# Where a wide expert unit's first two weight pieces land, and when they are transferred

## The reference

```python
def _swiglu(x, w_gate, w_up, w_down):
    return (jax.nn.silu(x @ w_gate) * (x @ w_up)) @ w_down

def _moe(h, w_router, w_gate, w_up, w_down):
    logits = (x @ w_router).astype(jnp.float32)
    top_v, top_i = lax.top_k(logits, TOP_K)          # TOP_K = 2 of 8 experts
    gates = jax.nn.softmax(top_v, axis=-1)
    combine = ...                                     # gate of each token and expert
    for e in range(N_EXPERTS):
        out = out + combine[:, e:e + 1] * _swiglu(x, w_gate[e], w_up[e], w_down[e])
```

## Time and profile before

| | us |
|---|---|
| median of three runs | 1407.58 (1405.72 to 1408.84) |
| the profiled execution's own time | 1405.3 |
| its span | 1403.5 |
| TensorE busy | 1325.2 (94%) |
| VectorE busy | 875.6 (62%) |
| ScalarE busy | 724.1 (52%) |
| mean transfer rate over the span | 314 GB/s, 440.55 MB |

### The profile page before, as it was taken

One profiled execution on the slowest core, in us unless ns is written; L12 is line 12 of the kernel. 1 busy time (PEld: TensorE's weight loads), 2 busy tenths in 40 slices (PEclk: granted clock), 3 DMA queues, 4 the chain that ended last, 5 costly groups with the idle time before them and its releaser, 6 DMA issues.

```text
span 1403.5 us, 19596 instructions
## 1 busy us (share of the span) xinstructions
PE 1325.2 (94%) x7528; PEld 1031.4 (73%) x7528; DVE 875.6 (62%) x954; ACT 724.1 (52%) x719; POOL 69.6 (5%) x92
## 2 busy tenths in 40 slices
PE   9999999999999999999997889998779998888997
PEld 8999999999999778888852258872238884226786
DVE  6554766544987699988830168860128881017897
ACT  7564544344566777777720057750027771006775
POOL 0100000000000063000000000000000000002000
PEclk9999999999999999999999999999999999999999
DMA  8563553553442799999989999989999999999992
GB/s 315 194 224 120 180 180 121 193 183 108 175 166 69 276 343 380 421 407 406 372 317 421 421 407 421 416 339 387 421 420 407 421 359 356 421 421 420 421 421 105
DMA packets 75877, 440.55 MB, mean 314 GB/s; under 512 B 7296, under 2 KB 9344, under 8 KB 30672
## 3 DMA queue, kind: packets, MB, share of 16 engines
q1 hardware_dynamic: 71680, 422.67, 76.4%
q0 software_dynamic: 3952, 16.49, 3.3%
q10 hardware_dynamic: 144, 0.02, 0.0%
HBM read 433.12 MB, written 11.01 MB: 316 GB/s over the span
## 4 chain that ended last, share of the span: by engine, by line
PE 72%; DMA 13%; DVE 7%; issue 4%; ACT 3%; SPq 0%; DVEq 0%; ACTq 0%
PE ps L2235 9%; PE ps L2236 9%; PE ps L2241 8%; DMA raw<-in_moe_w_gate 8%; PE ps L2360 7%; PE ps L1740 4%; PE ps L2259 4%; PE ps L2267 4%; PE ps L2260 4%; PE ps L1730 4%; PE ps L1731 4%; DMA raw<-in_moe_w_up 3%; PE ps L1778 2%; PE ps L1795 2%; PE ps L1779 2%
## 5 line engine op out<-in xcount | busy, mean ns | idle before, releaser
L1427 DVE TENSOR_TENSOR wl<-raw,wh 128x2048 fp32r<-128x2048 f32 x180 | 410.9, 2290 | 62.5 <-ACT wh L880 61.5
L880 ACT CAST wh<-raw 128x2048 fp32r<-128x2048 f32 x180 | 344.3, 1914 | 144.7 <-PE ps L2236 57.2
L2235 PE MATMUL ps<-wh,gh 128*128 128x512 f32 x560 | 222.0, 396 | 11.5 <-issue 8.4
L2236 PE MATMUL ps<-wh,gl 128*128 128x512 f32 x560 | 220.6, 394 | 0.0
L2360 PE MATMUL ps<-raw,few 128*64 128x512 f32 x288 | 139.3, 633 | 37.1 <-issue 28.7
L2362 PE MATMUL ps<-raw,few 128*64 128x512 f32 x312 | 155.8, 650 | 0.0
L2241 PE MATMUL ps<-wl,gh 128*128 128x512 f32 x560 | 151.3, 392 | 0.2 <-DVE wl L1427 0.2
L944 ACT ACTIVATE sil<-ps 64x512 f32<-64x512 f32 x21 | 12.4, 588 | 261.6 <-PE ps L2362 261.6
L2235 PEld LDWEIGHTS ps<-wh,gh 128*128 128x128 f32 x560 | 106.2, 190 | 37.3 <-issue 13.5
L2360 PEld LDWEIGHTS ps<-raw,few 128*64 128x64 f32 x288 | 39.2, 145 | 120.0 <-issue 120.0
L2236 PEld LDWEIGHTS ps<-wh,gl 128*128 128x128 f32 x560 | 106.2, 190 | 23.0
(11 more groups left out here) (353 smaller groups left out, 2378.2 us busy)
## 6 DMA issues: line engine op xcount, KB each, us to landing
raw<-in_moe_w_gate SPq DMA_DIRECT2D x101, 1024.0 KB, 11.3
raw<-in_moe_w_up SPq DMA_DIRECT2D x99, 1024.0 KB, 10.6
raw<-in_moe_w_down SPq DMA_DIRECT2D x88, 1024.0 KB, 12.1
raw_more<-in_moe_w_down SPq DMA_DIRECT2D x24, 1024.0 KB, 10.7
raw_more<-in_moe_w_up SPq DMA_DIRECT2D x13, 1024.0 KB, 14.1
raw<-in_diff_w_qkv SPq DMA_DIRECT2D x8, 1536.0 KB, 6.1
raw_more<-in_moe_w_gate SPq DMA_DIRECT2D x11, 1024.0 KB, 7.3
raw<-in_sb_w_qkv SPq DMA_DIRECT2D x7, 1536.0 KB, 7.7
```

Source lines behind the costliest of these rows:

```text
L880: act.copy(split_piece(wh, p), raw_piece(p)).then_inc(wh_ready, 1)
L1427: dve.tensor_tensor(split_piece(wl, p), raw_piece(p), raw_f(split_piece(wh, p)), ALU.subtract).then_inc(wl_ready, 1)
L2235: pe.matmul(ps[:, bank, :], gh[:, s], w, start=(k0 + k == 0), stop=False)
L2236: ins = pe.matmul(ps[:, bank, :], gl[:, s], w, start=False, stop=False)
```

## The change

The unused quarters of `wh` and `wl` get a second name, `unsplit`, by which float32 data can be written there. The first two pieces of each wide unit but the very first are transferred into them (`spare(0)` in `wh`, `spare(1)` in `wl`), with semaphores of their own (`spare_landed`). For the wide units behind small ones, the two transfers are issued by `load_few`, right behind its pieces 37 and 39, with no wait; pieces 2 to 41 still go to the raw slots. The counts of landings for each slot are changed to match. For the second wide unit the two are issued once the expert's number is known.

```diff
+        def splits(own):
+            return sb("wh", [P, 2, CHUNK], F32R, where=own), sb("wl", [P, 2, CHUNK], F32R, where=own)
+        wh, wl = phase(splits)
+        unsplit = phase(lambda own: sb("unsplit", [P, 2, 2, CHUNK], where=own))
...
+        def wide_piece(a, p, first=False):
+            if p < EARLY and not first:
+                return spare(p), spare_landed[p]
+            return raw_piece(p), piece_landed[p % RAW_SLOTS]
...
+            def load_early(a, e, p):
+                kind, i = unit_chunks[p // 2]
+                to, landed_ = wide_piece(a, p)
+                source = weights_of[kind][bass.ds(e * (FC * 2 * P) + P * (2 * i + p % 2), P), :]
+                sp.dma_start(to, source).then_inc(landed_, 16)
             def load_wide(a, e, few_before):
-                for p in range(PIECES):
+                for p in range(EARLY, PIECES):
                     kind, i = unit_chunks[p // 2]
                     if few_before is not None and p < RAW_SLOTS:
                         sp.wait_ge(few_used, few_before * PIECES + PIECES + p + 1 - RAW_SLOTS)
-                    else:
+                    elif p < RAW_SLOTS or p >= RAW_SLOTS + EARLY:
                         sp.wait_ge(wl_ready, a * PIECES + C_MOE + p + 1 - RAW_SLOTS)
                     load_piece(e, p, kind, i, p % 2)
-            def load_few(v, e):
+            def load_few(v, e, after):
...
                     load_piece(e, p, kind, i, half)
+                    if p in after:
+                        load_early(v + 1, after[p][0], after[p][1])
+            def early(e):
+                return {PIECES - 5: (e, 0), PIECES - 3: (e, 1)}
...
             with sp.Fori(1, len(SMALL_UNITS) + 1) as v:
-                load_few(v, sp.value_load(bm["unit_i"][0:1, bass.ds(2 * v, 1)], ...))
-                load_wide(v + 1, sp.value_load(bm["unit_i"][0:1, bass.ds(2 * v + 1, 1)], ...), v)
+                few_e = sp.value_load(bm["unit_i"][0:1, bass.ds(2 * v, 1)], ...)
+                next_e = sp.value_load(bm["unit_i"][0:1, bass.ds(2 * v + 1, 1)], ...)
+                load_few(v, few_e, early(next_e))
+                load_wide(v + 1, next_e, v)
...
-            def unit_split(u, a, p, first=False):
-                act.wait_ge(piece_landed[p % RAW_SLOTS], piece_in(u, p))
+            def unit_split(few, a, p, first=False):
+                piece, landed_ = wide_piece(a, p, first)
+                act.wait_ge(landed_, wide_in(a, few, p, first))
...
-                act.copy(split_piece(wh, p), raw_piece(p)).then_inc(wh_ready, 1)
+                act.copy(split_piece(wh, p), piece).then_inc(wh_ready, 1)
```

More of the change, by code:

```diff
@@ L95 @@
 RAW_SLOTS, SPLIT_SLOTS = 7, 3
+EARLY = 2
 MAX_UNITS = E + 4
@@ L293, in build @@
         piece_landed = [sem(f"piece_landed{i}") for i in range(RAW_SLOTS)]
+        spare_landed = [sem(f"spare_landed{i}") for i in range(EARLY)]
         wh_ready, wl_ready = sem("wh_ready"), sem("wl_ready")
@@ L406, in split_piece, with spare, landed_before, wide_in @@
             return w[:, slot // 2, slot % 2 * PIECE:(slot % 2 + 1) * PIECE]
-        def piece_in(u, p):
-            return u * (16 * PIECES // RAW_SLOTS) + 16 * (p // RAW_SLOTS + 1)
+        def spare(n):
+            return unsplit[:, n, SPLIT_SLOTS // 2, SPLIT_SLOTS % 2 * PIECE:(SPLIT_SLOTS % 2 + 1) * PIECE]
+        def wide_piece(a, p, first=False):
+            if p < EARLY and not first:
+                return spare(p), spare_landed[p]
+            return raw_piece(p), piece_landed[p % RAW_SLOTS]
+        def landed_before(slot, a, few):
+            rounds = PIECES // RAW_SLOTS
+            return 16 * rounds + 16 * (rounds - (1 if slot < EARLY else 0)) * (a - 1) + 16 * rounds * few
+        def wide_in(a, few, p, first=False):
+            if first:
+                return 16 * (p // RAW_SLOTS + 1)
+            if p < EARLY:
+                return 16 * a
+            slot = p % RAW_SLOTS
+            return landed_before(slot, a, few) + 16 * (p // RAW_SLOTS + (0 if slot < EARLY else 1))
+        def few_in(a, few, p):
+            return landed_before(p % RAW_SLOTS, a, few) + 16 * (p // RAW_SLOTS + 1)
         def split_free(a, p, first):
@@ L513, in _ @@
                     e = sp.value_load(bm["unit_i"][0:1, bass.ds(a + len(SMALL_UNITS), 1)], min_val=0, max_val=E - 1)
+                    for p in range(EARLY):
+                        load_early(a, e, p)
                     load_wide(a, e, None)
@@ L900, in _ @@
                          ps[:, BACKS[n], :]).then_inc(back_ev, 1)
-            unit_split(0, 0, 1)
+            unit_split(0, 0, 1, first=True)
             def gathered_high(k):
@@ L921, in _ @@
             gathered_high(1)
-            unit_split(0, 0, 2)
+            unit_split(0, 0, 2, first=True)
             def few_gathered(v):
@@ L979, in unit_body @@
                     if 2 * j + 3 < PIECES:
-                        unit_split(u, a, 2 * j + 3)
+                        unit_split(few, a, 2 * j + 3, first)
                     if kind == "d" and i + 1 < FC:
@@ L983, in unit_body @@
                     if 2 * j + 4 < PIECES:
-                        unit_split(u, a, 2 * j + 4)
+                        unit_split(few, a, 2 * j + 4, first)
                     if (kind, i) == ("g", 1):
@@ L1424, in unit_split @@
                 dve.wait_ge(wh_ready, a * PIECES + C_MOE + p + 1)
-                dve.wait_ge(w_used, split_free(a, p, first))
-                dve.tensor_tensor(split_piece(wl, p), raw_piece(p), raw_f(split_piece(wh, p)),
+                dve.wait_ge(w_used, split_free(a, p, first and p == 0))
+                dve.tensor_tensor(split_piece(wl, p), wide_piece(a, p, first)[0], raw_f(split_piece(wh, p)),
                                   ALU.subtract).then_inc(wl_ready, 1)
@@ L1493, in _ @@
             gathered_low(1, (0,))
-            unit_split(0, 1)
+            unit_split(0, 1, first=True)
             gathered_low(1, (1,))
-            unit_split(0, 2)
+            unit_split(0, 2, first=True)
             def sort_experts():
@@ L1635, in unit_body @@
                     if 2 * j + 3 < PIECES:
-                        unit_split(a, 2 * j + 3)
+                        unit_split(a, 2 * j + 3, first)
                     if kind == "u":
@@ L1648, in unit_body @@
                     if 2 * j + 4 < PIECES:
-                        unit_split(a, 2 * j + 4)
+                        unit_split(a, 2 * j + 4, first)
                     if stored and 8 <= j < 16:
```

51 lines of the change are left out of this document (27 added, 24 removed).

## The result

The changed kernel takes 1424.49 us (median of four runs, 1423.43 to 1425.19); the kernel before took 1407.57. The ratio is 1.0121, 95% interval [1.0103, 1.0138]: 16.9 us slower. Forecast were 1420 and a range of 1411 to 1425. The profiled execution took 1423.43 us with a span of 1421.4, against 1405.3 and 1403.5.

The account below looks back on a forecast made before the run. Transfers bound small units and TensorE wide ones; 5.65 + 5.65 + 1.7 at the three handovers gave 13.0 us, so 1418.3 on the profiled time, 1420.6 on the median, stated as 1420. Range 1411 to 1425.

Parts of the forecast that it names:

- Bound of the small unit: Small units are bound by transfers (DMA share 1.01); two early pieces make piece 41 land 5.0 us later.
- The hole ahead of piece 40 and its slow clock: Small unit's end: TensorE idles about 3.2 us before piece 40, whose matmuls then take about 3.3 us at 1.2 GHz.
- The refetch stays: First two handovers: refetching TensorE's loop code at the jump back keeps gaps of 4.16 and 4.28 us; +5.65 each.
- The sign that was to decide: First wide matmul of handover one to that of handover two: 230.4 us, was 224.76; below 227 would be wrong.
- The third handover: TensorE leaves its loop here; 1.3 us taken for that (bounds 0 to 2.28), so wide start +4.5 us.
- The last wide unit gives 2.8 back: Last wide unit: TensorE's waits for late pieces absorb 2.8 of the 4.5 us, leaving +1.7.
- Wide units give nothing back: Wide units at TensorE's pace, other than the last, absorb none of the handover delay, as no matmul there waits.
- the first: Rival: the handover gap closes, code fetched during the wait for piece 41; sum 0.4 to 3.4, 1408 to 1411; chance 0.12.
- the second: Rival: handover gap closes and piece 40 also finds a fast TensorE; -2.5 us in all, 1405.1; chance 0.06.
- the fourth: Rival: piece 41 lands at its old time; 1407 with the refetch, 1397 with the gaps closed too; chance 0.03.
- The third: Rival: nothing comes back in the last wide unit and slow stretches last longer; 17.5 us, 1425; chance 0.06.
- The rest is near zero: Remaining effects, such as first wide unit's early pieces, SyncE's second register load and casts reading other columns, cost near zero.

Follow-up runs that it names:

- the kernel with the old addresses: Changed kernel with wh and wl put back at their addresses of before, leaving only the early transfers, their waits and casts; 1416.07 us, ratio 1.0071.
- transfers_unrolled: Kernel before with only the early transfers changed (wh and wl at old addresses) and TensorE's loop written out; 1406.35 us, ratio 0.9992.
- layout_only: Kernel before with only wh and wl moved to the changed kernel's addresses (byte 88256 instead of 65664); 1414.23 us, ratio 1.005.

## Why the prediction was right, and by what luck

**Direction and range right, the sum right for a part of the cause.** The terms of the forecast belong to the kernel with the old addresses: 5.65 + 5.65 + 4.5 - 2.8 = 13.0. Measured there by stretch: 5.05 + 5.50 + 3.57 - 3.3 = 10.8, the whole difference of its span (1414.3 - 1403.5).

- Bound of the small unit: right. The DMA share stays at 1.01, and each early piece delays piece 41 by about one piece time. From the first small unit's start to piece 41's matmuls it is 98.80 us before, 101.38 with one early piece (+2.6) and 104.42 with two (+5.6, forecast 5.65).
- The hole ahead of piece 40 and its slow clock: right, 3.05 us against 3.2, and 3.34 us from piece 40's first matmul to piece 41's against 3.3. (The forecast's own addition slips here: 818.8 + 3.3 is 822.1, not 822.3.)
- The refetch stays: right in kind. With the loop written out the gap ends at the cast, and in the changed order it is gone. The size is less fixed than two rows of before (4.16 and 4.28) made it look: 3.40 to 4.84 over all kernels with a loop, 3.40 to 4.61 over those where the cast that TensorE needs was long done.
- The sign that was to decide, the period from the first handover to the second: forecast 230.4 us, 230.30 with the old addresses and 233.00 in the changed kernel. The 2.7 us between them are mostly the slower pace of a unit of 42 pieces, 1.8.
- The third handover: I took 1.3 us for leaving the loop, the low bound of 0 was right (1289.85 follows the last small matmul at once). The register load is covered.
- The last wide unit gives 2.8 back: 3.3 with the old addresses, 1.3 in the changed kernel, whose slower pace eats the rest.
- Wide units give nothing back: right for the changed kernel, but for the reason that I gave only in part. transfers_unrolled shows that they do give back what TensorE waited for transfers; in the kernel before, the refetch already took that slack.
- The rivals: the first and the second fall, since the gaps stayed (3.40 and 3.44) and piece 40 met a slow TensorE; the fourth falls, since piece 41 came late. The third, nothing given back and longer slow stretches, has the number (1425) but not the mechanism: with the old addresses 3.3 us came back.

**The step that failed** is "The rest is near zero. [...] Casts read other columns, same size". The diff moves the allocation of `wh` and `wl`, and I read it as a second name only. That term was costed at nothing without a row for it; alone it measures +7.8 us, nearly a half of the 16.9. The handovers came out lower than forecast (10.8) and the unseen term came on top, on opposite sides of 13.0, so that the total came out within 4 us. That is luck: 1424.49 lies above the 1415 to 1424 that the forecast gave its own mechanism, and half a microsecond inside the stated range.

One further difference isn't explained by a part: over its first 10 us wide unit 3 has a granted clock of 0.70 in the changed kernel against 0.84 before, and wide unit 4 has 1.00 against 0.83, though the idle times ahead of them are alike (3.40 and 3.44 us). Less the pace (1.8 us for 42 pieces), the units are 1.2 us longer and 1.7 shorter.

What stays open: why the place of wh and wl changes the pace. Offsets in 128 bytes and in 8 KB are excluded; 65664 is fast, 68864, 88064, 88256 and 90240 are slow. Meeting the writes of ScalarE and VectorE is made unlikely by the intervals above; meeting the transfers that land elsewhere in the partition was not tested. Five places with one fast among them don't give a rule, whether it is wh or wl or both isn't known, and other blocks (16 or 32 KB), or the place relative to the tokens' buffers, were not tried.

## What to carry to other kernels

In a stretch bound by transfers, fetching one piece early only delays what stands behind it; put it where the queue idles, and look whether the issuing engine is free there, its own loop's jump included. When a wait is taken away, write down what was hidden in its shadow (here a refetch of 4 us, and behind that the transfers of the next pieces) before counting a gain. And when a diff moves a buffer's allocation, compare the pace of the engine that reads it first, in a stretch where nothing else has changed.

## What the runs showed of the hardware that I had not expected

- The pace of float32r matmuls with a moving operand of 128x512 changed with the place of that operand in its partition, at a granted clock of 1.00: 2.748 us for a piece of twelve with wh at 65664, 2.79 to 2.80 at four other places, 1.5 to 2%, some 3 to 4 ns for each matmul. VectorE's and ScalarE's times hardly change (before against layout_only: 2290 and 2289 ns for a subtraction, 1914 and 1907 for a cast).
- At its jump back to the loop's top TensorE is idle for 3.4 to 4.6 us where nothing else holds it, with one 16 KB instruction packet in the gap; leaving the loop costs nothing that can be seen. At SyncE's jump the time between the same two issues, with two register loads in each, is 7.69 and 7.24 us against 1.95 and 1.94 without a jump.
